# A two-layer decoder step: the first expert search of each tail split by head, and the other groups' queries spread over the expert slots

## The reference, cut to what matters

```python
def _peer(x, w_q, sub_keys, u_tab, v_tab):
    q = (xt @ w_q).reshape(n, PEER_HEADS, 2, PEER_HALF)              # 8 heads
    s = jnp.einsum('nhck,hcmk->nhcm', q, sub_keys)                   # 128 keys a half
    ts, ti = lax.top_k(s, PEER_TOPK)                                 # 16 of 128, twice
    cand_s = ts[:, :, 0, :, None] + ts[:, :, 1, None, :]             # 256 pairs
    best_s, best_p = lax.top_k(cand_s, PEER_TOPK)                    # 16 of 256
    idx = take(cand_i, best_p); gate = softmax(best_s)
    a = gelu(einsum(x, u_tab[idx])) * gate
    return einsum(a, v_tab[idx])

def _tail(x, p, ...):
    x = x + _peer(_rmsnorm(x, norm_ffn), ...)
    gate = sigmoid(_rmsnorm(x, norm_ple) @ ple_gate)
    return x + gate * (p @ ple_proj)
```

## Time and profile before

| what | value |
|---|---|
| median of three runs | 2385.8 us |
| the profiled execution | 2396.1 us, its span 2394.3 us |
| PE busy | 1991.2 us (83%) |
| DVE busy | 1294.3 us (54%) |
| ACT busy | 753.5 us (31%) |
| POOL busy | 649.5 us (27%) |
| queue of the gathers (q0) | 662.74 MB, 66.7% of the 16 DMA engines' span |
| mean TensorE clock granted | 0.934 of full speed |
| first gather of tail 0, of tail 1 | at 369.64 us, at 1626.64 us |

### The profile page before, as it was taken

One profiled execution on the slowest core, in us unless ns is written; L12 is line 12 of the kernel. 1 busy time (PEld: TensorE's weight loads), 2 busy tenths in 40 slices (PEclk: granted clock), 3 DMA queues, 4 the chain that ended last, 5 costly groups with the idle time before them and its releaser, 6 DMA issues. The chain is left out here.

```text
span 2394.3 us, 25072 instructions
## 1 busy us (share of the span) xinstructions
PE 1991.2 (83%) x8710; PEld 956.0 (40%) x8710; DVE 1294.3 (54%) x3280; ACT 753.5 (31%) x2211; POOL 649.5 (27%) x650
## 2 busy tenths in 40 slices
PE   7799778887878888866999999888888888888765
PEld 5577645322223332222435554555322223332221
DVE  4486846477667766754100211036477667766754
ACT  3200012444344444443101221122444344444443
POOL 0000003444444344431010000103444444444441
PEclk9897778999999999977999999998999999999987
DMA  9999957999999999996997777827999999999995
GB/s 310 367 332 344 352 192 287 408 426 427 427 427 426 426 416 427 427 426 277 379 372 266 281 298 301 308 110 290 399 426 427 427 426 427 426 427 427 427 427 220
DMA packets 123903, 874.96 MB, mean 365 GB/s; under 512 B 19742, under 2 KB 29727, under 8 KB 38776
## 3 DMA queue, kind: packets, MB, share of 16 engines
q0 software_dynamic: 92160, 662.74, 66.7%
q1 hardware_dynamic: 30751, 198.03, 22.8%
q10 hardware_dynamic: 864, 12.58, 1.4%
HBM read 861.99 MB, written 118.81 MB: 410 GB/s over the span
## 5 line engine op out<-in xcount | busy, mean ns | idle before, releaser
L1489 PE MATMUL tail_acc<-tail_ring,tail_diag 128*128 128x512 f32 x1248 | 616.2, 622 | 135.6 <-ACT tail_diag L1346 134.6
L1631 POOL DMA_INDIRECT tail_ring<-in_peer_uv,tail_idx x348 | 366.3, 1053 | 893.9 <-PE tail_acc L1489 473.1
L1234 DVE CUSTOM_DVE_ANT_0 tail_ring<-tail_ring,all_h 128x1024 f32<-128x1024 f32 x348 | 423.9, 1223 | 236.7 <-DMA tail_ring<-in_peer_uv,tail_idx 234.8
L1489 PE MATMUL tail_acc<-mid_wring,tail_diag 128*128 128x512 f32 x800 | 393.8, 622 | 76.4 <-ACT tail_diag L1346 76.0
L1489 PEld LDWEIGHTS tail_acc<-tail_ring,tail_diag 128*128 128x128 f32 x1248 | 220.5, 192 | 516.6 <-ACT tail_diag L1346 329.7
L1234 DVE CUSTOM_DVE_ANT_0 mid_wring<-mid_wring,all_h 128x1024 f32<-128x1024 f32 x228 | 278.2, 1223 | 181.8 <-DMA mid_wring<-in_peer_uv,tail_idx 181.6
L1340 ACT ACTIVATE tail_gelus<-tail_dots 128x1 f32<-128x1 f32 x576 | 116.3, 202 | 732.4 <-DVE tail_dots L1234 732.2
L1631 POOL DMA_INDIRECT mid_wring<-in_peer_uv,tail_idx x228 | 245.2, 1075 | 320.6 <-PE tail_acc L1489 273.1
L1752 PE MATMUL mix_acc<-mid_wring,all_hT 128*128 128x512 f32 x576 | 276.4, 615 | 1.5 <-PEq L80 1.4
L1489 PEld LDWEIGHTS tail_acc<-mid_wring,tail_diag 128*128 128x128 f32 x800 | 143.5, 193 | 315.3 <-ACT tail_diag L1346 195.2
L1346 ACT ACTIVATE tail_diag<-all_ident,tail_weights 128x128 f32<-128x128 f32 x512 | 205.5, 401 | 22.5 <-PE tail_acc L1489 6.0
(11 more groups left out here) (359 smaller groups left out, 2010.3 us busy)
## 6 DMA issues: line engine op xcount, KB each, us to landing
mid_wring<-in_w_qkv SPq DMA_DIRECT2D x18, 2048.0 KB, 9.7
mix_ring<-in_kT POOLq DMA_DIRECT2D x16, 1024.0 KB, 9.8
mix_ring<-in_v_rows POOLq DMA_DIRECT2D x16, 1024.0 KB, 9.8
out_kv_s<-in_cache_kv_w SPq DMA_DIRECT2D x8, 2016.0 KB, 70.5
mix_ring<-in_kT POOLq DMA_DIRECT2D x16, 768.0 KB, 10.9
mix_ring<-in_v_rows POOLq DMA_DIRECT2D x16, 768.0 KB, 9.5
mid_wring<-in_w_ab ACTq DMA_DIRECT2D x4, 2048.0 KB, 27.7
tail_w_big<-in_w_query SPq DMA_DIRECT2D x8, 1024.0 KB, 12.1
```

Of the source, the lines that this page charges most:

```text
L1234: V.tensor_tensor_reduce(out=u, in0=u, in1=h[:, g, :], scale=1.0, scalar=0.0, op0=ALU.mult, op1=ALU.add, accum_out=dots[:, n:n + 1]).then_ ...
L1489: last = mm(acc[g][:, c * 512:(c + 1) * 512], diag[:, n % DIAGS, :], v[:, c * 512:(c + 1) * 512], start=first, stop=final)
L1631: pool.indirect_dma_start(slot(r), None, table, bass.IndirectOffsetOnAxis(ap=idx[:, j, i:i + 1], axis=0)).then_inc(landed[r], 16)
```

## The change

The first pair's search is done one head at a time. `search_head(0)` works on scores that `scores_head(0)` writes to `acc[1]` as soon as head 0's query is copied; `search_head(1)` has the same steps on scores in `ps`. Each has its own marks for the row numbers, so POOL may gather slots 0 to 15 after head 0's search. `queries` now lists group 0's 128 columns of all eight heads first, and then the other 160 columns of all eight. Ahead of slot 0 only queries 0 to 3 remain; 4 to 7 stand behind slots 1, 3, 5, 7, and 8 to 15 behind slots 12, 20, ..., 68. Group 1's addition, norm and scaling move on DVE from ahead of slot 0 to behind slots 3 and 4, its transpose on PE behind slot 9. No search steps run beside slots 0 and 1.

```diff
+QUERY_AT = {1: 4, 3: 5, 5: 6, 7: 7, **{12 + 8 * i: 8 + i for i in range(PH)}}
-        queries = [(0, 0, 128), (1, 0, 128), (0, 128, NTOK), (1, 128, NTOK)] + [(n, 0, NTOK) for n in range(2, PH)]
+        first_score = lambda i, c: (ps if i else acc[1])[:, c * 512:c * 512 + NKEY]
+        queries = [(n, 0, 128) for n in range(PH)] + [(n, 128, NTOK) for n in range(PH)]
 # search, with the same change at the two waits on exp_ready
-                    dve.wait_ge(score_ready, j + 1)
+                    dve.wait_ge(score_ready, j + 2)
+                def search_head(i):
+                    s = lambda m: first_score(i, m % 2)
+                    mine = slice(i * TOPK, (i + 1) * TOPK)
+                    pair = (2 * i, 2 * i + 1)
+                    dve.wait_ge(score_ready, i + 1)
...
+                    mark["scores_read", 0 if i else "first"] = ch.n
...
+                    mark["exp", 0, i] = ch.n
...
+                    mark["idx", 0, i] = ch.n
+                def gate_head(i):
+                    mine = slice(i * TOPK, (i + 1) * TOPK)
+                    dve.wait_ge(exp_ready, i + 1)
+                    ch(V.reciprocal(total[:, 0, i:i + 1], total[:, 0, i:i + 1]))
+                    ch.step(V.tensor_scalar(gate[:, 0, mine], be[:, 0, i, :], total[:, 0, i:i + 1], None, ALU.mult))
+                    mark["gate", 0, i] = ch.n
 # DVE
-                for _ in search(0):
-                    pass
-                exp_after[0] = -1
-                add_out(1, 0)
-                add_out(1, 1)
-                square_sum("ffn", 1)
-                mean("ffn", 1)
-                scaled("ffn", 1)
+                search_head(0)
+                search_head(1)
+                gate_head(0)
+                gate_head(1)
...
-                        for _ in range(3):
+                        for _ in range(3 if n >= 2 else 0):
...
                         dot_product(n)
+                        if n == 3:
+                            add_out(1, 0)
+                            add_out(1, 1)
+                            square_sum("ffn", 1)
+                            mean("ffn", 1)
+                        if n == 4:
+                            scaled("ffn", 1)
 # ACT
+                exps_head(0)
                 copy_columns("ffn", 2)
-                exps(0)
-                root("ffn", 1)
-                copy_columns("ffn", 1)
-                for i in range(2, 6):
-                    copy_query(i)
+                exps_head(1)
+                copy_query(2)
+                copy_query(3)
...
-                    if n in (2, 4, 6, 8):
-                        copy_query(5 + n // 2)
+                    if n == 3:
+                        root("ffn", 1)
+                    if n == 10:
+                        copy_columns("ffn", 1)
+                    if n - 1 in QUERY_AT:
+                        copy_query(QUERY_AT[n - 1])
 # PE
+                def scores_head(i):
...
+                    pe.wait_ge(q_copied, i + 1)
+                    for c in range(2):
+                        r = slice(c * 64, c * 64 + 64)
+                        last = mm(first_score(i, c), qT[r, i, 0:128], keysT[r, i, :], start=True, stop=True)
+                    last.then_inc(score_ready, 1)
...
                 query(0)
+                scores_head(0)
                 query(1)
-                scores(0)
+                scores_head(1)
+                pe.wait_ge(dve_steps, mark["scores_read", "first"])
                 project_out(1, 0)
                 turn("ffn", 2)
                 project_out(1, 1)
-                turn("ffn", 1)
-                for i in range(2, 6):
-                    query(i)
+                query(2)
+                query(3)
                 scores(1)
...
                     weighted_sum(n)
-                    if n in (1, 3, 5, 7):
-                        query(6 + n // 2)
+                    if n == 9:
+                        turn("ffn", 1)
+                    if n in QUERY_AT:
+                        query(QUERY_AT[n])
 # POOL
-                    if i == 0:
+                    if j == 0 and i % TOPK == 0:
+                        pool.wait_ge(dve_steps, mark["idx", 0, i // TOPK])
+                    elif i == 0:
                         pool.wait_ge(dve_steps, mark["idx", j])
```

More of the change, by code:

```diff
@@ L1190, in search @@
                     if j >= 2:
-                        dve.wait_ge(exp_ready, j - 1)
+                        dve.wait_ge(exp_ready, j)
                     ch.step(V.tensor_tensor(be[:, j % 2], bs[:], over(bs[:, :, 0], 2, TOPK), ALU.subtract))
@@ L1221, in search @@
                     yield from rest(3)
-                    dve.wait_ge(exp_ready, j + 1)
+                    dve.wait_ge(exp_ready, j + 2)
                     ch(V.reciprocal(total[:, j % 2], total[:, j % 2]))
@@ L1226, in search @@
                     mark["gate", j] = ch.n
+                def search_head(i):
[3 more added lines that the diff above has]
+                    dve.wait_ge(score_ready, i + 1)
+                    for m in pair:
+                        ch.step(V.max(ts[:, m, 0:8], s(m)))
+                    for m in pair:
+                        ch.settle(lag=1)
+                        ch.step(V.match_replace(sc[:, m, :], ts[:, m, 0:8], s(m), NEG))
+                    for m in pair:
+                        ch.settle(lag=1)
+                        ch.step(V.max(ts[:, m, 8:16], sc[:, m, :]))
+                    for m in pair:
+                        ch.step(V.max_index(ti[:, m, 0:8], ts[:, m, 0:8], s(m)))
+                    mark["scores_read", 0 if i else "first"] = ch.n
+                    for m in pair:
+                        ch.settle(lag=3)
+                        ch.step(V.max_index(ti[:, m, 8:16], ts[:, m, 8:16], sc[:, m, :]))
+                    ch.step(V.tensor_tensor(cand[:, i, :].rearrange("q (a b) -> q a b", a=TOPK),
+                                            over(ts[:, 2 * i, :], 2, TOPK), over(ts[:, 2 * i + 1, :], 1, TOPK), ALU.add))
+                    ch.settle(lag=1)
+                    ch.step(V.tensor_copy(tif[:, 2 * i:2 * i + 2, :], ti[:, 2 * i:2 * i + 2, :]))
+                    ch.settle(lag=1)
+                    ch(V.max(bs[:, i, 0:8], cand[:, i, :]))
+                    ch(V.match_replace(cand2[:, i, :], bs[:, i, 0:8], cand[:, i, :], NEG))
+                    ch.step(V.max(bs[:, i, 8:16], cand2[:, i, :]))
+                    ch.step(V.max_index(bp[:, i, 0:8], bs[:, i, 0:8], cand[:, i, :]))
+                    ch.settle(lag=1)
+                    ch.step(V.max_index(bp[:, i, 8:16], bs[:, i, 8:16], cand2[:, i, :]))
+                    ch.step(V.tensor_tensor(be[:, 0, i, :], bs[:, i, :], over(bs[:, i, 0], 1, TOPK), ALU.subtract))
+                    mark["exp", 0, i] = ch.n
+                    ch.settle(lag=1)
+                    ch.step(V.tensor_scalar(part[:, 0, mine], bp[:, i, :], 4, None, ALU.logical_shift_right))
+                    ch.step(V.tensor_scalar(part[:, 1, mine], bp[:, i, :], 15, None, ALU.bitwise_and))
+                    ch.settle()
+                    ch(V.tensor_copy(partf[:, :, mine], part[:, :, mine]))
+                    for half in range(2):
+                        ch.step(V.tensor_tensor(hot[:, half, mine, :], over(partf[:, half, mine], 2, TOPK),
+                                                over(iota[:], 1, TOPK), ALU.is_equal))
+                    for half in range(2):
+                        ch.settle(lag=1)
+                        ch.step(V.tensor_tensor(hot[:, half, mine, :], hot[:, half, mine, :],
+                                                over(tif[:, 2 * i + half, :], 1, TOPK), ALU.mult))
+                    for half in range(2):
+                        ch.settle(lag=1)
+                        ch.step(V.tensor_reduce(rowf[:, half, mine], hot[:, half, mine, :], AX_X, ALU.add))
+                    ch.settle()
+                    ch.step(V.scalar_tensor_tensor(out=idx[:, 0, mine], in0=rowf[:, 0, mine], scalar=float(NKEY),
+                                                   in1=rowf[:, 1, mine], op0=ALU.mult, op1=ALU.add))
+                    mark["idx", 0, i] = ch.n
@@ L1333, in exps, with exps_head @@
                     last.then_inc(exp_ready, 1)
+                def exps_head(i):
+                    act.wait_ge(dve_steps, mark["exp", 0, i])
+                    A(be[:, 0, i, :], be[:, 0, i, :], ACT.Exp, accum_out=total[:, 0, i:i + 1]).then_inc(exp_ready, 1)
                 def weigh(n):
@@ L1340, in weigh @@
                     ch(A(gelus[:, n:n + 1], dots[:, n:n + 1], ACT.Gelu))
-                    if i == 0:
+                    if j == 0 and i % TOPK == 0:
+                        act.wait_ge(dve_steps, mark["gate", 0, i // TOPK])
+                    elif i == 0:
                         act.wait_ge(dve_steps, mark["gate", j])
@@ L1453, in query @@
                         pe.wait_ge(q_copied, i - 1)
-                    pe.wait_ge(hT_ready, 1 if hi == 128 else 3)
```

(12 more changed lines are left out.)

## The result

The changed kernel takes 2357.65 us (median of four runs, 2355.98 to 2360.63) against 2386.09 us: ratio 0.9881, 95% interval 0.9868 to 0.9894, so 28.4 us faster (25 to 32). The forecast was 2355 us, 31 us faster. The profiled execution took 2358.0 us, its span 2356.2 us.

The account below looks back on a forecast made before the run. Tails were taken as bound by DMA bytes, the first gather's start and later DMA shortage. Savings of 16.2 and 17.0 us, less 1 a tail, total 31.2: from 2385.8 to 2355 us, own range 2349 to 2363.

Parts of the forecast that it names:

- The shortage: Early in each tail's slots, DMA transfer lost while gathers wait for PE: 8.2 and 9.0 us, all saved.
- The start of the gather: Opening of each tail: searching one head first brings the first gather 8.0 us earlier (6.6 to 9.1).
- What the start is worth: Both tails: a microsecond saved on the first gather's start reaches the tail's end, so 8.0 us a tail.
- tail 0's: Sum for tail 0: 8.0 us of start plus 8.2 of shortage, 16.2, before 1 us taken off.
- The 1 us a tail off for slowed gathers: Openings: 1 us a tail deducted because the first gathers are issued while DVE is busy with head 1.
- Rival 2: Openings: first gathers' descriptors held until head 1's search ends, so only the shortage goes; 2370 us, chance 0.03.
- the gather at 371.05: Tail 0 before the change: POOL's gather ran through DVE operations, 1.87 us not 0.94, read as slowed, not stopped.
- Rival 1: Tail slots: only the start is gained, the shortage stays through late norm or exponentials; 2371 us, chance 0.10.
- Rival 3: Tail slots: PE's clock stays at 1.2 GHz, slots take 3.43 us; slower, 2408 us, chance 0.03.
- Rival 4: No change: freed transfers are taken back elsewhere, for instance by w_gate at slot 68; 2386 us, chance 0.04.
- The slack at slot 4: Gather 14 waits for slot 4's matmul, done about 387, and isn't due before 402: nearest miss 13 us away.
- w_gate costs the same in either place: Gate weights' load moved behind slot 68: its 4.2 MB cost 9.8 us of transfer in either place.

Follow-up runs that it names:

- after_again: The changed kernel itself, run and profiled again beside other runs: 2354.14 us, ratio 0.9874 to the kernel before.
- e5: Changed kernel with queries 4 to 7 ahead of slot 0 instead of behind slots 1, 3, 5 and 7: 2358.85 us, 0.9893 of the kernel before.
- e4: Changed kernel with group 1's addition, norm and scaling back ahead of slot 0 on DVE: 2355.4 us, 0.9884 of the kernel before.
- e7: Changed kernel with group 0's following norm taken 8 slots later: 2356.6 us, 0.9879 of the kernel before.
- e9: Changed kernel plus e7's step, head 0's first 8 row numbers written early, and group 0's scaling to query 0 in halves: 2351.95 us, 0.9855 of the kernel before.
- e8: e6's kernel, but SP holds the gate weights' two loads until slot 68: 2383.64 us, 0.9989 of the kernel before.
- e6: Changed kernel with all sixteen queries, group 1's norm and its transpose ahead of slot 0: 2370.36 us, 0.9931 of the kernel before.
- e1: Kernel before with only the search done head by head, queries and group 1's norm left in their old places: 2385.99 us, ratio 1.0000.

## Why the prediction was right, and where its sizes were off

The mechanism held: both terms are there, and each was forecast in its place. The rates show them apart. These are three stretches behind the first query, 0 to 22 us, 22 to 50 and 50 to 100, before in tail 0 and then after; the last two rows are the third stretch of tail 1, before and after:

```profile
350.26:372.26 22.00, 18.68 (x74) 10.34 (x74) 17.27 (x71) 4.07 (x10) 2.32 (x2) 1.00 0.08 24
372.26:400.26 28.00, 21.35 (x86) 16.19 (x87) 9.24 (x31) 6.64 (x16) 9.63 (x10) 0.77 1.01 393
400.26:450.26 50.00, 48.69 (x146) 26.38 (x145) 30.46 (x78) 18.46 (x61) 19.10 (x19) 0.99 0.90 357
346.15:368.15 22.00, 21.08 (x93) 12.83 (x94) 18.88 (x84) 3.02 (x10) 7.27 (x8) 1.00 0.41 150
368.15:396.15 28.00, 25.98 (x125) 16.43 (x124) 20.42 (x64) 14.03 (x40) 12.20 (x12) 1.00 1.02 398
396.15:446.15 50.00, 44.87 (x140) 21.09 (x138) 32.12 (x64) 22.45 (x69) 22.18 (x21) 1.00 1.01 427
1657.28:1707.28 50.00, 48.31 (x147) 26.34 (x146) 31.15 (x83) 18.49 (x62) 22.79 (x19) 1.00 0.90 348
1637.08:1687.08 50.00, 46.09 (x147) 22.50 (x146) 32.23 (x65) 23.00 (x71) 22.02 (x21) 1.00 1.01 427
```

- The shortage, forecast at 8.2 and 9.0 us: the third stretch had (427 - 357) / 427 x 50 = 8.2 us and 9.3 us of transfer missing, and has none after. That term was right in both tails, in this profile; in `after_again` the stretch had 416 and 425 GB/s, 1.3 and 0.2 us missing.
- The start of the gather: 8.0 us forecast, 8.2 measured (19.38 - 11.22). The search from first maximum to row numbers took 357.08 - 349.23 = 7.85 us, forecast 8.1; its start, counted from the first query, was right to 0.2.
- What the start is worth was put a little too high. The first stretch misses 20.8 us of transfer before and 14.3 after: 6.5 us, and 7.1 in tail 1. One part of the difference is in the rows: before, SP's copies began with the first gather and moved 0.38 MB, 0.9 us of transfer, by 372.0, when no gathered row had moved yet. These copies come after the gathers now, so that much of the start was not idle before.
- The term of the sum that was mis-sized is tail 0's: 15.2 us forecast, 12.6 measured (11.8 in `after_again`); tail 1's was 16.0, with 15.8 and 13.5 measured. Behind the opening the prediction had put nothing. There tail 0 loses (427 - 418 + 427 - 360) / 427 x 20 = 3.6 us in 800 to 840 against 1.4 before (397 GB/s in one such stretch), so 2.2 us of it. Its size scatters (377 GB/s in the changed kernel's other profile, 392 in e5, 346 in e4). That it arises from group 0's following norm beside the next search's last steps is what e7's profile speaks for; e9 doesn't bear it out, so the cause isn't shown.
- The 1 us a tail off for slowed gathers was not needed: the ten gathers of the opening took 0.94 to 1.11 us, the row at 362.51 one of them, while DVE was 9.76 of 10 us busy. Here luck helped: without these 2 us the sum is 33.2 us against 28.4 measured, so a loss that did not occur stood in for part of one that the sum had left out.
- Rival 2, all of it held, is excluded: the first gather is issued at 357.37, 7 us before head 1's row numbers. But the prediction's reading that the gather at 371.05 was slowed and not stopped was wrong: it began 0.17 us into a square sum of 1.23 us and ended 0.81 us behind it. A gather is held to the end of such an operation, as the last section shows; it is each hold that is short.
- Rival 1 (the exponentials and the norm again late) is excluded: no wait of that size is left, and e4 has even more of DVE ahead of slot 0 at no cost. Rival 3 is excluded: 1.00 granted in each stretch from 355 to 435. Rival 4 is excluded by the time, and by 427 GB/s where 357 and 348 stood.
- Slot 0 at 372.51, corrected by 4.11 us 376.6, was forecast at 377. The slack at slot 4 I gave as 13 us, though its own numbers, 402 and 387, are 15 apart; at gather 10 it is some 15, and e5, e4 (inside) and e8 (beyond) bear that out. Rivals 1 and 2 had 1 us taken off in all where the forecast took 1 a tail, which decides nothing.
- That w_gate costs the same in either place holds only while the queues are full; e6 against e8 (13 us) shows its other value, which the prediction did not have.
- That a microsecond of the start is worth one, whatever else, was put too broadly: e1 has the full 8 us of start and gains 0.0.

## What to carry to other kernels

Behind a ring of buffers, an earlier first transfer is worth only as much as the consumer's first release comes within the ring's reach: measure both, the start and the first release, and move the later one first. Work ahead of the first release is free as long as the transfers of one full ring, and what else the queues have to move, last. By an estimate from these runs that was ten gathers of 2.455 us and 5 us of SP's copies, some 30 us behind the first gather; e8 gives 17.4 + 15, some 32. If a hole can't be closed, put other transfers that are needed anyway into it.

## What the runs showed of the hardware

A gather's issue on POOL took 0.94 us unless it began inside an operation of DVE that reads two operands from SBUF, the on-chip memory of the tiles outside PSUM; then it lasted until that operation's end and 0.81 us beyond. In tail 0 of the changed kernel the 153 gathers begun while DVE was idle took 0.93 to 0.95 us. Those begun inside a dot of 1.22 us took 0.94 to 1.97, each what the dot had left plus 0.81 and at least 0.94, within 0.02; only one begun in the dot's first 0.04 us took 0.93. These rows have a long operation, a short one, and an addition whose second operand lies in PSUM, beside which the gather at 374.74 took 0.94:

```profile
363.23 0.75 DVE L1273 TENSOR_TENSOR tail_one_hot<-tail_one_hot,tail_top_at_f 128x256 f32<-128x256 f32 x2
363.75 1.04 POOL L1717 DMA_INDIRECT tail_ring<-in_peer_uv,tail_idx  x1 [0.31 <-issue]
374.60 1.28 DVE L1121 TENSOR_TENSOR all_x<-all_x,tail_acc 128x512 f32<-128x512 f32 x2
375.92 1.22 DVE L1081 CUSTOM_DVE_ANT_0 all_h<-all_x 128x1024 f32<-128x1024 f32 x1
376.46 1.50 POOL L1717 DMA_INDIRECT tail_ring<-in_peer_uv,tail_idx  x1 [0.78 <-PE tail_acc L1570]
```

By the Trainium skill (SBUF — State Buffer, "Who interferes with whom") DVE operations with two inputs in SBUF contend with GpSimd's reads. These rows agree, for the long operation and for the short one. The holds cost nothing in the slots, since a transfer lasts 2.455 us: in e6 DVE was 10.00 of 10 us busy from 410 to 420, gathers took up to 2.02 us, and the rate was 428 GB/s.
